# Delta rule in one core: 16x16 diagonal blocks of the inverse by substitution on GpSimd in three of four steps

## The chip, the cores and the metric

The kernel runs on one core of a Trainium2 chip. The metric is the device time of one execution in microseconds (us), lower is better; several runs are timed and their median is taken. Engines are called as in the profile: PE is TensorE, DVE VectorE, ACT ScalarE, POOL GpSimd, SP SyncE, which here only issues DMAs.

## The reference, cut to what matters

The program is two large blocks, one after the other, over 1024 tokens of width 1024: a hybrid of a gated delta rule and dilated attention with a feed-forward part, then a block with two state space branches. Only one piece of the delta rule is touched, run forwards and backwards over the tokens, for 8 heads of 64 values:

```python
kb = k * beta[..., None]
a_low = jnp.where(strict, jnp.einsum('nhcid,nhcjd->nhcij', kb, k) * decay, 0.0)
tmat = lax.linalg.triangular_solve(eye + a_low, eye, left_side=True, lower=True, unit_diagonal=True)
u = jnp.einsum('nhcij,nhcjv->nhciv', tmat, v * beta[..., None])
w = jnp.einsum('nhcij,nhcjk->nhcik', tmat, kb * jnp.exp(g)[..., None])
# then, chunk by chunk: v_new = u - w S; o = q S + (q k^T) v_new; S = decay S + k^T v_new
```

So each chunk needs the inverse `tmat` of a unit triangular matrix I + A. The kernel takes chunks of 128 tokens, so A and its inverse are 128x128.

## The kernel before, in words

Heads are taken in 4 pairs, p = 0 to 3. A pair has 8 chunks in each direction d. A group n = 8 p + s holds chunk s of both directions and both heads, four 128x128 matrices, in a tile that is 128x512. Two groups, called e = 0 and 1, are worked on together; that is a step, m = 0 to 3, so a pair has four steps and the kernel sixteen.

For each pair PE first does four projections of 1024x1024 by 128 columns, the blocks `dn` 0 to 3 (`product`, L303; each matmul is made three times from a high and a low part of its operands, and POOL makes those parts of each weight block in `split`, L249 and L251). Small work of the pair before and of this one is hooked in between their matmuls. Then come the four steps, in which PE does no projection.

Preparation of a group: POOL spreads the log decays (`spread`, L1967), PE sums them (`spread_g`, L1309), DVE and ACT form the exponentials (`exponents`, `exponential`), PE makes k k^T and q k^T (`gram`, L1325), DVE multiplies by the decay (`decayed`), PE transposes (`turn_a`, L1336) and ACT scales into the tile AA (`take_a`, L1610). POOL then forms X = I - A within 2x2 blocks (`first_level`, L1975 and L1979), PE transposes it (`turn_x0`, L1346) and ACT copies it to YY (`take_y0`).

The inverse is then built in NL = 6 levels. Level l turns diagonal blocks of size 2, 4, ... 64 into blocks of twice the size: PE multiplies A by Y (`times_a`, L1364, or L1361 at the last level), DVE masks the product into PM (`masked`, L1803), PE multiplies by X (`times_x`, L1390), DVE subtracts from Y (`corrected`). From level 1 on X is Y transposed anew (`turn_y`, L1377, and ACT's `take_x`, L1623).

Each level of a step has two slots, q = 2 l and 2 l + 1, one behind `times_a` and one behind `times_x`. A function `between(p, m, q)` on PE, ACT and DVE puts other work there: at q = 0 to 5 of steps 1 to 3 the scan of the two groups of the step before (`scan1`, `scan2`, `scan3`: L1264 and L1269, L1281, L1290 and L1297), and at q = 0 to 11 of steps 0 to 2 the preparation of the next step's two groups. Every engine runs its list in order and waits on semaphores. SP's list has only weight loads in this stage; a load waits until POOL has split the block that had the buffer before.

## Time and profile before

| | us |
|---|---|
| median of 3 runs | 3808.23 |
| the runs | 3802.79 to 3814.48 |
| the profiled execution: its own time | 3801.48 |
| the profiled execution: its span | 3799.7 |

| engine | busy us | share of the span |
|---|---|---|
| PE matmul | 3641.7 | 96% |
| PE weight load | 3016.4 | 79% |
| DVE | 1549.1 | 41% |
| POOL | 1297.7 | 34% |
| ACT | 1070.8 | 28% |

The shares are means over the whole program. A time like 1211.88 in the rows further down is us from the start of the span. In a timeline neighbouring instructions of one line are merged: a row gives the start, the time from the start of the first to the end of the last, the count, and in brackets how long the engine was idle before and who released it. Ends of matmuls are modelled and overlap the next start, so distances between starts are used here.

### The profile page before, as it was taken

What the parts mean: (1) busy time and instruction counts of PE and PEld (TensorE: products, weight loads), DVE (VectorE), ACT (ScalarE), POOL (GpSimd) and SP (SyncE); (2) the same over time, 40 slices, a digit from 0 to 9 for tenths busy, and PEclk for the clock granted to TensorE, in tenths of its full rate; (3) what the DMA queues carried; (4) which work ended last, traced back from release to release, by engine and by line L of the source; (5) the groups of instructions that cost most, each with busy time, mean ns of one, the idle gap of its engine ahead of it and who ended that gap; (6) DMA issues with size and microseconds to landing.
All of it is one profiled execution on the core that took longest, in us unless ns stands there. A gap on an engine that the chain in (4) does not pass through costs nothing. (4 is left out here: it accounts for less than half of the span.)

```text
span 3799.7 us, 47903 instructions
## 1 busy us (share of the span) xinstructions
PE 3641.7 (96%) x19176; PEld 3016.4 (79%) x19176; DVE 1549.1 (41%) x2391; ACT 1070.8 (28%) x1817; POOL 1297.7 (34%) x876
## 2 busy tenths in 40 slices
PE   6999999999999999999999999999979999999998
PEld 5777878776898989888877787887867887777877
DVE  4332333343354535444574333333337224444433
ACT  3343333331333333333013111111121114443221
POOL 4221212124221221222345343433342435554543
PEclk9999999999999999999999999999989999999999
DMA  2000000002000000001131111111132111111122
GB/s 98 23 29 27 28 23 33 24 28 76 29 12 12 1 23 1 23 1 60 67 127 59 50 44 50 44 50 44 50 116 70 48 43 49 48 47 46 61 83 72
DMA packets 52699, 173.19 MB, mean 46 GB/s; under 512 B 6569, under 2 KB 13353, under 8 KB 49841
## 3 DMA queue, kind: packets, MB, share of 16 engines
q1 hardware_dynamic: 52528, 170.80, 13.1%
q8 instruction: 122, 2.00, 0.2%
q14 instruction: 49, 0.39, 0.0%
HBM read 151.25 MB, written 19.52 MB: 45 GB/s over the span
## 5 line engine op out<-in xcount | busy, mean ns | idle before, releaser
L303 PE MATMUL DP<-XH,WH 128*128 128x512 f32 x2608 | 896.4, 425 | 21.7 <-POOL WL L251 20.5
L249 POOL CAST WH<-WRAW 128x1024 fp32r<-128x1024 f32 (+2 forms) x257 | 263.8, 1026 | 1638.3 <-issue 1041.5
L303 PE MATMUL DP<-XL,WH 128*128 128x512 f32 x2608 | 812.3, 393 | 0.0
L303 PE MATMUL DP<-XH,WL 128*128 128x512 f32 x2608 | 810.3, 392 | 0.0
L303 PEld LDWEIGHTS DP<-XH,WH 128*128 128x128 f32 x2608 | 475.0, 191 | 180.5 <-issue 86.8
L251 POOL TENSOR_TENSOR WL<-WRAW,WH 128x1024 fp32r<-128x1024 f32 (+2 forms) x257 | 588.5, 2290 | 20.7
L303 PEld LDWEIGHTS DP<-XL,WH 128*128 128x128 f32 x2608 | 494.2, 190 | 107.2
L303 PEld LDWEIGHTS DP<-XH,WL 128*128 128x128 f32 x2608 | 492.7, 189 | 107.1
L836 DVE SCALAR_TENSOR_TENSOR SS<-B,RQ,SBI 128x256 f32<-128x256 f32 (+2 forms) x192 | 74.5, 429 | 380.7 <-PE B L541 380.7
L1975 POOL TENSOR_TENSOR XX<-AA,CON 128x256 f32<-128x256 f32 x64 | 45.4, 731 | 433.4 <-ACT AA L1610 433.4
L1390 PE MATMUL DP<-PM,XX 128*128 128x64 f32 (+1 forms) x1536 | 172.6, 269 | 15.4 <-ACT XX L1623 15.0
L1390 PEld LDWEIGHTS DP<-PM,XX 128*128 128x128 f32 (+1 forms) x1536 | 163.2, 184 | 29.2 <-issue 26.3
L686 ACT ACTIVATE PP<-SS,NM 128x256 f32<-128x256 f32 (+2 forms) x192 | 88.4, 461 | 317.4 <-DVE NM L843 317.4
L1364 PEld LDWEIGHTS DP<-YY,AA 128*128 128x128 f32 x1280 | 151.2, 192 | 13.9 <-issue 13.1
L1364 PE MATMUL DP<-YY,AA 128*128 128x64 f32 x1280 | 156.0, 275 | 4.3 <-ACT YY L1617 4.3
L1623 ACT ACTIVATE XX<-DP 128x512 f32<-128x512 f32 x160 | 86.8, 594 | 237.8 <-PE DP L1377 237.8
L367 DVE TENSOR_TENSOR XR<-XR,B 128x1024 f32<-128x1024 f32 x88 | 106.4, 1219 | 101.5 <-PE B L347 101.5
L2135 DVE SCALAR_TENSOR_TENSOR TG<-DP,COL,TG 128x1023 f32<-128x1023 f32 x44 | 56.5, 1283 | 196.6 <-ACT TG L2123 193.8
L1803 DVE TENSOR_TENSOR PM<-DP,CM 128x256 f32<-128x256 f32 x192 | 81.5, 425 | 129.9 <-PE DP L1364 127.2
L541 PE MATMUL B<-KZA,QA 128*128 128x512 f32 (+2 forms) x192 | 130.6, 768 | 0.0
L2135 DVE SCALAR_TENSOR_TENSOR TU<-DP,COL,TU 128x1023 f32<-128x1023 f32 x44 | 56.4, 1283 | 173.8 <-ACT TU L2123 170.9
L347 PE MATMUL B<-FH,WH 128*128 128x512 f32 x352 | 109.7, 393 | 15.5 <-DVE XR L367 15.5
(461 smaller groups left out, 5497.9 us busy)
## 6 DMA issues: line engine op xcount, KB each, us to landing
WRAW<-in_w_up SPq DMA_DIRECT2D x44, 512.0 KB, 3.2
WRAW<-in_w_attn SPq DMA_DIRECT2D x36, 512.0 KB, 3.2
WRAW<-in_w_down SPq DMA_DIRECT2D x22, 512.0 KB, 3.2
XR<-in_x SPq DMA_DIRECT2D x8, 1024.0 KB, 8.0
WRAW<-in_w_dn SPq DMA_DIRECT2D x16, 512.0 KB, 3.5
WRAW<-in_w_lrux SPq DMA_DIRECT2D x10, 512.0 KB, 3.3
WRAW<-in_w_lrug SPq DMA_DIRECT2D x10, 512.0 KB, 3.2
WRAW<-in_w_bl SPq DMA_DIRECT2D x10, 512.0 KB, 3.5
```

What stands on the lines that cost most here:

```text
L249: pool.tensor_copy(WH[b.slot][:, 0:b.kt, :], WRAW[b.slot][:, 0:b.kt, :]).then_inc(w_hi, 1)
L251: pool.tensor_tensor(WL[b.slot][:, 0:b.kt, :], WRAW[b.slot][:, 0:b.kt, :], WH[b.slot][:, 0:b.kt, :].bitcast(F32), ALU.subtract).then_inc(w ...
L303: mm = pe.matmul(DP[b.slot][:, half * H:half * H + H], w[b.slot][:, k, :], x[:, k, half * H:half * H + H], start=one, stop=end)
L347: mm = pe.matmul(dst[:, half * H:half * H + H], w[b.slot][:, k0 + k, :], x[:, k, half * H:half * H + H], start=one, stop=end)
L367: dve.tensor_tensor(dst[:, m0 + o, :], dst[:, m0 + o, :], (B45, B67)[o % 2][:, :], ALU.add).then_inc(part_read, 1)
L541: pe.matmul(SPS[t % 2][:, 0:2 * w].rearrange("p (h k) -> p h k", h=2), att_tokens(g, t)(QA[i % 2][:, :]), keys, start=True, stop=True).the ...
L686: e = act.activation(PP[t % 2][:, h, 0:w], SS[t % 2][:, h, 0:w], ACT.Exp, scale=0.125, bias=NM[:, g, t, o:o + 1], accum_out=LS[:, g, t, o: ...
L1364: mm = pe.matmul(PT_U[e][:, o:o + 64].rearrange("p (m b) -> p m b", b=2 << l), AA[v][e][:, d, h, :], part(YY[v][e][:, d, h, :], l, 1 - d), ...
L1390: mm = pe.matmul(PT_U[e][c, o:o + 64], XX[v][e][c, d, h, c], PM[e][c, d, h, :], start=True, stop=True)
L1623: act.activation(XX[v][e][:, :, :, :].rearrange("p d h n -> p (d h n)"), PT_X[e], ACT.Copy).then_inc(lx_ready[e], 1)
L1803: dve.tensor_tensor(PM[e][:, :, :, :], PT_U[e][:, 0:256].rearrange("p (d h n) -> p d h n", d=2, h=2), CM[:, l].rearrange("p d (a n) -> p d ...
L2135: dve.scalar_tensor_tensor(out=d, in0=src, scalar=COL[:, ds(f * 2 + (COLS["ffnconv"] + 44 * tap + 22 * part + t), 1)], in1=d, op0=ALU.mult ...
```

## The change

In step 0 of each pair the inverse is built as before, in six levels. In steps 1 to 3 `lowest(n)` is NB = 3: levels 0 to 2 are left out, and levels 3 to 5 start from the inverses of the 16x16 diagonal blocks. These come over a new path, once per step, for the 64 blocks of its two groups:

1. SP (`blocks_sp`) waits for `take_a` of both groups, writes AA (512 KB) to `aa_dram` and waits for its landing.
2. SP issues 8 DMAs of the diagonal blocks back, each 8 blocks of 16 rows of 64 bytes, so that a block lies in one partition of BL or BW.
3. POOL (`base_blocks`) inverts all 64 blocks at once: four instructions of layout, 14 times a multiply and a subtract, and one more of layout. Each waits for the one before it.
4. SP issues 8 DMAs of the blocks into the diagonal of `yy_dram`, waits for them, waits for the scans that still read the YY tile, and loads `yy_dram` (512 KB) into YY. The first `times_a` of the step waits for it.

`first_level`, `turn_x0` and `take_y0` are left for step 0 only. With six slots instead of twelve in steps 1 to 3, the preparation moves: slots 0 to 10 of step 0 make the matrices of steps 1 and 2, step 1 makes those of step 3, and steps 2 and 3 only scan. AA has three buffers instead of two, the q k^T tiles eight instead of six, XX one instead of two. SP has the two first loads of the next pair ahead of the three paths. DVE zeroes a tile that SP writes to `yy_dram` once, behind `st_zero` of pair 0 and ahead of two weight loads. The last fills of MX change places.

```diff
@@ -1059,10 +1059,15 @@
...
-        AA = [[at(f"AA{v}{e}", 112 + 4 * v + 2 * e, [P, 2, 2, P]) for e in range(2)] for v in range(2)]
-        XX = [[at(f"XX{v}{e}", 120 + 4 * v + 2 * e, [P, 2, 2, P]) for e in range(2)] for v in range(2)]
...
+        AAV = [at(f"AA{v}", kb, [P, 2, 2, 2, P]) for v, kb in enumerate((120, 116, 148))]
+        YYV = [at(f"YY{v}", S0 + 38 + 4 * v, [P, 2, 2, 2, P]) for v in range(2)]
...
+        XX = [at(f"XX{e}", S0 + 34 + 2 * e, [P, 2, 2, P]) for e in range(2)]
+        BL, BY, BT, BW = (at(n, 124 + i, [P, 16, 16]) for i, n in enumerate(("BL", "BY", "BT", "BW")))
+        aa_dram = nc.dram_tensor("aa_dram", [P, 8, P], F32, kind="Internal").ap()
+        yy_dram = nc.dram_tensor("yy_dram", [P, 8, P], F32, kind="Internal").ap()
...
@@ -1123,7 +1132,53 @@
...
+        def lowest(n):
+
+            return 0 if n // 2 % 4 == 0 else NB
...
+        def diagonal(dram, q):
+
+            return bass.AP(dram.tensor, dram.offset + P * q, ap=[[16 * (8 * P + 1), 8], [8 * P, 16], [1, 16]])
+
+        def blocks_sp(sp, g):
+
+            c, v, m = chain(g), g % 2, g % 4
+            sp.wait_ge(aa_ready, 2 * g + 2)
+            sp.dma_start(aa_dram, AAV[m][:, :, :, :, :].rearrange("p d e h n -> p (d e h) n")).then_inc(aa_out, 16)
+            sp.wait_ge(aa_out, AA0 + 16 * (c + 1))
+            sp.wait_ge(yy_out, YYO0 + 128 * c)
+            for q in range(8):
+                t = BW if q >= 4 else BL
+                sp.dma_start(t[8 * q:8 * q + 8, :, :], diagonal(aa_dram, q)).then_inc(blk_in, 16)
+            if c:
+                sp.wait_ge(yy_in, YYI0 + 16 * c)
+            sp.wait_ge(blk_ready, RDY0 + c + 1)
+            for q in range(8):
+                t = BW if q >= 4 else BY
+                sp.dma_start(diagonal(yy_dram, q), t[8 * q:8 * q + 8, :, :]).then_inc(yy_out, 16)
+            sp.wait_ge(yy_out, YYO0 + 128 * (c + 1))
+            sp.wait_ge(v_ps, 2 * g - 2)
+            sp.dma_start(YYV[v][:, :, :, :, :].rearrange("p d e h n -> p (d e h) n"), yy_dram).then_inc(yy_in, 16)
...
@@ -1169,13 +1224,13 @@
...
-            sp.dma_start(MX[:, 2:4, :], mx_dram[:, 2:4, :]).then_inc(mx_in[1], 16)
+            for i in range(2):
...
-            sp.dma_start(MX[:, 4:6, :], mx_dram[:, 4:6, :]).then_inc(mx_in[2], 16)
...
             sp.wait_ge(qkv_ready, NGRP)
-            sp.dma_start(MX[:, 0:2, :], mx_dram[:, 0:2, :]).then_inc(mx_in[0], 16)
+            sp.dma_start(MX[:, 4:6, :], mx_dram[:, 4:6, :]).then_inc(mx_in[2], 16)
...
@@ -1339,38 +1396,40 @@
...
             def times_a(n, l):
                 p, s, e, v = grp(n)
                 if l == 0:
-                    pe.wait_ge(y0_ready, n + 1)
-                if n // 2 * NL + l:
-                    pe.wait_ge(ly_ready[e], n // 2 * NL + l)
+                    pe.wait_ge(y0_ready, n // 8 * 2 + e + 1)
+                elif l == lowest(n):
+                    pe.wait_ge(yy_in, YYI0 + 16 * (chain(n // 2) + 1))
+                if levels_done(n, l):
+                    pe.wait_ge(ly_ready[e], levels_done(n, l))
...
@@ -1493,32 +1552,35 @@
                         scan2(a + 1)
                     if q == 5:
                         scan3(a + 1)
-                if m < 3:
-                    n = NT * p + 2 * m + 2
-                    if q == 0:
-                        spread_g(n)
+                n = NT * p + 2 * m + 2
+                if m == 0 and q < 11:
+                    i, k = q // 6 * 2, q % 6
+                    if k == 0:
+                        spread_g(n + i)
+                        spread_g(n + i + 1)
+                    if k in (2, 3):
+                        gram(n + i, k - 2)
+                    if k == 4:
+                        turn_a(n + i)
+                        turn_a(n + i + 1)
+                if m == 1:
                     if q == 1:
-                        spread_g(n + 1)
-                    if q == 3:
-                        gram(n, 0)
+                        spread_g(n + 2)
+                        spread_g(n + 3)
+                    if q in (3, 4):
+                        gram(n + 2, q - 3)
                     if q == 5:
-                        gram(n, 1)
-                    if q == 7:
-                        turn_a(n)
-                        turn_a(n + 1)
-                    if q == 10:
-                        turn_x0(n)
-                    if q == 11:
-                        turn_x0(n + 1)
+                        turn_a(n + 2)
+                        turn_a(n + 3)
             for p in range(NPAIR):
                 if p:
                     for e in range(2):
-                        pe.wait_ge(lx_ready[e], 5 * 4 * p)
+                        pe.wait_ge(lx_ready[e], TV * p)
                 product(pe, Block("dn", p, 0), XH, XL, within=scans_first(p))
                 if p:
                     for e in range(2):
-                        pe.wait_ge(ly_ready[e], NL * 4 * p)
+                        pe.wait_ge(ly_ready[e], LV * p)
                 product(pe, Block("dn", p, 1), XH, XL, within=scans_last(p))
                 product(pe, Block("dn", p, 2), XH, XL, within=during_v(p))
                 product(pe, Block("dn", p, 3), XH, XL, within=during_z(p))
@@ -1529,19 +1591,20 @@
...
                 for m in range(4):
                     a = NT * p + 2 * m
-                    for l in range(NL):
+                    for l in range(lowest(a), NL):
+                        q = 2 * (l - lowest(a))
                         times_a(a, l)
                         times_a(a + 1, l)
                         if l:
                             turn_y(a, l)
                             turn_y(a + 1, l)
-                        between(p, m, 2 * l)
+                        between(p, m, q)
                         times_x(a, l)
                         times_x(a + 1, l)
-                        between(p, m, 2 * l + 1)
+                        between(p, m, q + 1)
...
@@ -1907,6 +1976,8 @@
...
+                if p == 0:
+                    dve.memset(YYV[1][:, :, :, :, :], 0.0)
                 dve.memset(SB[:, :, :], 0.0).then_inc(st_zero, 1)
...
@@ -1960,24 +2032,56 @@
                 p, s, e, v = grp(n)
                 if n >= 2:
-                    pool.wait_ge(dec_ready, 2 * n - 2)
+                    pool.wait_ge(dec_ready, 4 * (n // 2))
                 for d in range(2):
                     i = 8 * d + 2 * p
                     g = ABN[:, chunk(s, d), i:i + 2].rearrange("p (h k) -> p h k", k=1).broadcast_to([P, 2, P])
                     x = pool.tensor_tensor(RB[e][:, d], twice(con("tri", d, P)), g, ALU.mult)
                 x.then_inc(rb_ready, 1)
+            def step(p, c, i):
+
+                return 2 * (p + 1) + NSTEP * c + i
+
             def first_level(n):
                 p, s, e, v = grp(n)
+                k = step(p - 1, 3 * p, e + 1)
                 pool.wait_ge(aa_ready, n + 1)
                 for d in range(2):
-                    x = pool.tensor_tensor(XX[v][e][:, d], AA[v][e][:, d], twice(con("m0", d, P)), ALU.mult)
+                    x = pool.tensor_tensor(XX[e][:, d], aa(n)[:, d], twice(con("m0", d, P)), ALU.mult)
                 x.then_inc(x0_part, 1)
-                pool.wait_ge(x0_part, n + 1)
+                pool.wait_ge(x0_part, k)
                 for d in range(2):
-                    x = pool.tensor_tensor(XX[v][e][:, d], twice(IDENT), XX[v][e][:, d], ALU.subtract)
+                    x = pool.tensor_tensor(XX[e][:, d], twice(IDENT), XX[e][:, d], ALU.subtract)
                 x.then_inc(x0_ready, 1)
+
+            def base_blocks(g):
+
+                p, c = g // 4, chain(g)
+                lo, up = slice(0, 32), slice(32, 64)
+                pool.wait_ge(blk_in, BLK0 + 128 * (c + 1))
+                pool.tensor_scalar(BY[lo, :, :], BL[lo, :, :].rearrange("p i j -> p j i"), -1.0, None, ALU.mult).then_inc(
+                    blk_step, 1)
+                pool.wait_ge(blk_step, step(p, c, 1))
+                pool.wait_ge(rb_ready, min(NT * p + 2 * (g % 4) + 4, NGRP))
+                pool.tensor_scalar(BY[up, :, :], BW[up, :, :], -1.0, None, ALU.mult).then_inc(blk_step, 1)
+                pool.tensor_copy(BL[up, :, :], BW[up, :, :].rearrange("p i j -> p j i")).then_inc(blk_step, 1)
+                pool.wait_ge(blk_step, step(p, c, 3))
+                pool.tensor_copy(BY[0:64, :, :].rearrange("p i j -> p (i j)")[:, 0:256:17], ONES[0:64, 0:16]).then_inc(
+                    blk_step, 1)
+                pool.wait_ge(blk_step, step(p, c, 4))
+                for j in range(1, 15):
+                    y = BY[0:64, 0:j, j + 1:16]
+                    t = BT[0:64, 0:j, j + 1:16]
+                    pool.tensor_tensor(t, BY[0:64, 0:j, j:j + 1].broadcast_to([64, j, 15 - j]),
+                                       BL[0:64, j + 1:16, j:j + 1].rearrange("p i a -> p a i").broadcast_to(
+                                           [64, j, 15 - j]), ALU.mult).then_inc(blk_step, 1)
+                    pool.wait_ge(blk_step, step(p, c, 2 * j + 3))
+                    pool.tensor_tensor(y, y, t, ALU.subtract).then_inc(blk_step, 1)
+                    pool.wait_ge(blk_step, step(p, c, 2 * j + 4))
+                pool.tensor_copy(BW[up, :, :], BY[up, :, :].rearrange("p i j -> p j i")).then_inc(blk_ready, 1)
+                pool.wait_ge(blk_ready, RDY0 + c + 1)
             def add_other(n):
@@ -2007,12 +2104,20 @@
...
-                for m in range(4):
-                    prepare(NT * p + 2 * m)
-                add_other(NT * p + 4)
-                add_other(NT * p + 5)
                 for i in range(2):
+                    first_level(NT * p + i)
+                for i in range(2, 4):
+                    spread(NT * p + i)
+                for m in range(1, 4):
+                    for n in range(NT * p + 2 * m + 2, min(NT * p + 2 * m + 4, NGRP)):
+                        spread(n)
+                    base_blocks(4 * p + m)
+                for i in range(2):
+                    if i:
+                        for e in range(2):
+                            pool.wait_ge(lp_ready[e], levels_done(NT * p + 4 + e, NL))
                     split(pool, Block("dn", p + 1, i) if p < NPAIR - 1 else Block("mixga", 0, i))
+                    add_other(NT * p + 4 + i)
...
@@ -2534,11 +2639,18 @@
                     load(sp, Block("dn", 0, i), a["w_dn"])
                     mx_spill(sp, 6 + i)
                 sp.dma_start(CM[:, :, :, :], a["levels"]).then_inc(cm_in, 16)
+                sp.wait_ge(st_zero, 1)
+                sp.dma_start(yy_dram, YYV[1][:, :, :, :, :].rearrange("p d e h n -> p (d e h) n")).then_inc(yy_out, 16)
                 for p in range(NPAIR):
-                    for i in range(0 if p else 2, 4):
+                    for i in range(2, 4):
                         load(sp, Block("dn", p, i), a["w_dn"])
-                for i in range(2):
-                    load(sp, Block("mixga", 0, i), a["w_gatea"], i)
+                    for i in range(2):
+                        if p < NPAIR - 1:
+                            load(sp, Block("dn", p + 1, i), a["w_dn"])
+                        else:
+                            load(sp, Block("mixga", 0, i), a["w_gatea"], i)
+                    for m in range(1, 4):
+                        blocks_sp(sp, 4 * p + m)
                 mx_fill(sp)
                 for i, w in enumerate(("w_dnout", "w_gatea")):
                     load(sp, Block("mixa", 0, i), a[w], 2 * i)```

SP's list in pair 0, before. Behind these rows only weight loads follow up to the fills of MX.

```order
L241 DMA WRAW_54<-in_w_dn 128x1024
L1166 DMA mx_dram<-GB_101 128x1024
L2536 DMA CM<-in_levels 128x768
L241 DMA WRAW_53<-in_w_dn 128x1024
L241 DMA WRAW_54<-in_w_dn 128x1024
```

The same list now, from the second pair of weight loads on, the path of step 1 and the beginning of that of step 2.

```order
L241 DMA WRAW_53<-in_w_dn 128x1024
L241 DMA WRAW_54<-in_w_dn 128x1024
L1167 DMA aa_dram<-AA_121 128x1024
L1172 DMA BL<-aa_dram 8x16x16 x4
L1172 DMA BW<-aa_dram 8x16x16 x4
L1178 DMA yy_dram<-BY 8x16x16 x4
L1178 DMA yy_dram<-BW 8x16x16 x4
L1181 DMA YY_124<-yy_dram 128x1024
L1167 DMA aa_dram<-AA_122 128x1024
```

A path is 18 DMAs in one list, and the next path stands behind the last of them.

PE's list in pair 0, before: the last level of step 0 and the first of step 1. XX_126 and XX_127 are what `first_level` made for step 1.

```order
L1361 MATMUL DP<-YY_128,AA_120 64x64 x4
L1361 MATMUL DP<-YY_129,AA_121 64x64 x4
L1377 MATMUL DP<-CON,YY_128 128x128 x4
L1377 MATMUL DP<-CON,YY_129 128x128 x4
L1346 MATMUL B<-CON,XX_126 128x128 x4
L1390 MATMUL DP<-PM_138,XX_124 64x64 x4
L1390 MATMUL DP<-PM_139,XX_125 64x64 x4
L1346 MATMUL B<-CON,XX_127 128x128 x4
L1364 MATMUL DP<-YY_130,AA_122 128x64 x4
L1364 MATMUL DP<-YY_131,AA_123 128x64 x4
```

The same place now. YY_124 is the tile that SP loads, and the row with it is the first of step 1.

```order
L1420 MATMUL DP<-YY_123,AA_120 64x64 x8
L1436 MATMUL DP<-CON,YY_123 128x128 x8
L1393 MATMUL B<-CON,DQX 128x128 x8
L1449 MATMUL DP<-PM_137,XX_125 64x64 x4
L1449 MATMUL DP<-PM_138,XX_126 64x64 x4
L1423 MATMUL DP<-YY_124,AA_121 128x64 x8
L1436 MATMUL DP<-CON,YY_124 128x128 x8
L1319 MATMUL B<-SB,KQ 128x128 x2
L1324 MATMUL B<-SB,KQ 128x128 x2
```

The last level of step 0 now holds the `turn_a` of step 2 (L1393), the `turn_x0` are gone, and the first scan stands behind the row that waits.

## Rows read from the trace of the kernel before

**Rows 1.** Windows, pair 1: length; PE, PEld, DVE, ACT, POOL busy; clock; DMA share, GB/s.
```profile
1211.88:1245.86 33.98, 32.46 (x272) 29.65 (x273) 15.27 (x41) 10.76 (x23) 8.15 (x13) 0.95 0.00 1
1245.86:1283.32 37.46, 36.63 (x331) 34.45 (x329) 20.27 (x63) 14.94 (x41) 7.89 (x13) 1.00 0.00 1
1283.32:1320.78 37.46, 36.63 (x330) 34.45 (x329) 20.28 (x63) 13.99 (x40) 7.90 (x13) 1.00 0.01 1
1320.78:1352.73 31.95, 30.75 (x290) 29.67 (x289) 14.91 (x46) 10.29 (x29) 10.99 (x10) 1.00 0.10 34
```

**Rows 2.** Timeline of PE, levels 1 to 5 of step 3, pair 1.
```profile
1326.15 1.95 PE L1364 MATMUL DP<-YY,AA 128*128 128x64 f32 x16
...
1332.83 1.90 PE L1364 MATMUL DP<-YY,AA 128*128 128x64 f32 x16
...
1339.41 1.95 PE L1364 MATMUL DP<-YY,AA 128*128 128x64 f32 x16
...
1342.59 1.97 PE L1390 MATMUL DP<-PM,XX 128*128 128x64 f32 x16 [0.34 <-ACT XX L1623]
1344.39 1.95 PE L1364 MATMUL DP<-YY,AA 128*128 128x64 f32 x16
...
1349.47 1.03 PE L1361 MATMUL DP<-YY,AA 64*64 64x64 f32 x16
...
1352.73 0.73 PE L303 MATMUL DP<-XH,WH 128*128 128x512 f32 x2
```

**Rows 3.** Timeline of PE, step 0 of pair 1.
```profile
1218.00 1.08 PE L1309 MATMUL B<-RB,CON 128*128 128x256 f32 x4
1218.91 1.89 PE L1364 MATMUL DP<-YY,AA 128*128 128x64 f32 x16
...
1223.93 1.14 PE L1325 MATMUL B<-KQ 64*128 64x256 f32 x8
1225.00 2.00 PE L1364 MATMUL DP<-YY,AA 128*128 128x64 f32 x16
...
1236.20 1.04 PE L1336 MATMUL B<-CON,DQX 128*128 128x128 f32 x8
1237.09 1.90 PE L1364 MATMUL DP<-YY,AA 128*128 128x64 f32 x16
```

**Rows 4.** Timeline of ACT, the same step.
```profile
1236.85 2.18 ACT L1610 ACTIVATE AA<-B,PSC 128x128 f32<-128x128 f32 x8 [2.11 <-PE B L1336]
```

**Rows 5.** DMA issues by line: count, KB each, median us to landing.
```profile
WRAW<-in_w_attn SPq DMA_DIRECT2D x36, 512.0 KB, 3.2
...
mx_dram<-GB SPq DMA_DIRECT2D x8, 512.0 KB, 2.9
...
MS<-kp_dram SPq DMA_DIRECT2D x64, 32.0 KB, 1.9
...
kp_dram<-KS SPq DMA_DIRECT2D x8, 32.0 KB, 1.6
```

**Rows 6.** Timeline of SP, DMAs issued one behind another.
```profile
2864.68 7.62 SPq L2715 DMA_DIRECT2D MS<-kp_dram  x16
```

**Rows 7.** Groups of POOL, shapes apart: count, busy us, mean ns, idle before.
```profile
L1975 POOL TENSOR_TENSOR XX<-AA,CON 128x256 f32<-128x256 f32 x64 | 45.4, 731 | 433.4 <-ACT AA L1610 433.4
...
L1989 POOL TENSOR_TENSOR OQ<-OQ,OD 128x128 f32<-128x128 f32 x32 | 14.0, 458 | 153.0 <-ACT OQ L1580 153.0
...
L926 POOL TENSOR_SCALAR SBI<-BX,CON 128x256 f32<-128x256 f32 x8 | 7.4, 932 | 0.0
...
L249 POOL CAST WH<-WRAW 128x256 fp32r<-128x256 f32 x10 | 5.0, 498 | 10.7 <-PE DP L303 10.7
```

**Rows 8.** Timeline of POOL, L1979 waits for the result of L1975.
```profile
1030.72 1.42 POOL L1975 TENSOR_TENSOR XX<-AA,CON 128x256 f32<-128x256 f32 x2 [23.91 <-ACT AA L1610]
1032.21 1.41 POOL L1979 TENSOR_TENSOR XX<-CON,XX 128x256 f32<-128x256 f32 x2
```

**Rows 9.** Timeline of PE, its return after an idle stretch in another stage.
```profile
2789.23 1.19 PE L333 MATMUL DP<-XH,WH 128*128 128x512 f32 x2 [4.98 <-POOL XL L444]
```

**Rows 10.** Windows, the stretch behind that return.
```profile
2789.23:2793.60 4.37, 4.37 (x10) 3.44 (x11) 2.45 (x2) 1.88 (x2) 4.22 (x2) 0.50 0.87 375
```

More of the change, by code:

```diff
@@ L1720, in delta_act @@
                     a = NT * p + 2 * m
-                    for l in range(NL):
+                    for l in range(lowest(a), NL):
+                        q = 2 * (l - lowest(a))
                         if l:
@@ L1939, in delta_dve @@
                     a = NT * p + 2 * m
-                    for l in range(NL):
+                    for l in range(lowest(a), NL):
+                        q = 2 * (l - lowest(a))
                         masked(a, l)
                         masked(a + 1, l)
-                        between(p, m, 2 * l)
+                        between(p, m, q)
                         corrected(a, l)
                         corrected(a + 1, l)
-                        between(p, m, 2 * l + 1)
+                        between(p, m, q + 1)
             a, b = NGRP - 2, NGRP - 1
```

139 lines of the change are left out of this document (78 added, 61 removed).

## The prediction

> **What bounds the kernel now.** I read the windows of the four steps of one pair first, then the timeline of PE inside a step, then who feeds it. In the four steps of pair 1 PE is busy 136.5 of 140.85 us (33.98 + 37.46 + 37.46 + 31.95), DVE, ACT and POOL at most 54% of any step [rows 1]. The timeline shows the same from within: PE goes from one list item to the next and waits only 0.34 us per level, for ACT's copy of the transposed X [rows 2]. So a step costs what PE's instructions cost, and no projection runs beside it. Whatever leaves PE's list in a step shortens the program, as long as nothing later than PE takes over. The other pairs look alike, so I work out pair 1 and take it four times.
>
> **What PE's list loses.** Step 3 has only scans between its levels. Its six levels take, by distances between `times_a` starts, 5.37 (from 1320.78, where the last window of [rows 1] begins, to 1326.15), 6.68, 6.58, 4.98, 5.08 and 3.26 us [rows 2]. Level 2 has scan work and level 3 has none but a 0.34 us wait, so one level's scan work is 6.58 - 4.98 + 0.34 = 1.94. Eight transposes take 0.89 (1236.20 to 1237.09), two matmuls of `spread_g` for one group 0.91 (1218.00 to 1218.91), a `gram` 1.07 (1223.93 to 1225.00) [rows 3].
>
> - New steps 2 and 3: the first level with a `turn_y` that level 0 did not need, 5.37 + 0.89; then 6.68; then the small last level with scans in its slots, 3.26 - 0.34 + 1.94. Sum 17.8.
> - New step 1: the same and one preparation, 2 x 0.91 + 2 x 1.07 + 0.89 = 4.85. Sum 22.7.
> - New step 0: 33.98, less `turn_x0` (0.89), plus the second preparation (4.85). Sum 37.9.
>
> PE's work is then 96.2 us a pair instead of 140.85, 44.7 less. If nothing took over, the program would lose 179 us.
>
> **What takes over: the path through memory.** Call L the time from `take_a` of a step to YY landed. Nothing in it is PE's, and SP and POOL do it in order. Its parts:
>
> - AA out, 512 KB: 2.9 to landing, as `mx_dram<-GB` [rows 5].
> - 8 DMAs of blocks in: SP issues 16 DMAs in 7.62 us, 0.476 each [rows 6], so the last is issued 3.3 behind the first, and lands 1.9 later, as `MS<-kp_dram` [rows 5]. 5.2.
> - POOL, below: 12.5.
> - 8 DMAs out: 3.3, and 1.6 as `kp_dram<-KS` [rows 5]. 4.9.
> - YY in, 512 KB: 3.2 as the weight loads [rows 5].
> - Five handovers between SP, DMA and POOL, of which the trace shows only one kind, POOL to itself (0.07, below). I take 0.6 for all.
>
> POOL runs 28 dependent instructions of 14 to 56 elements, 1120 in all. No such small one is in the trace. 128x256 takes 0.731 and 128x128 0.458 [rows 7], so 2.13 ns an element and 0.185 fixed. A dependent one starts 0.07 behind the end of its predecessor (1030.72 + 1.42 = 1032.14, next at 1032.21) [rows 8]. So 28 x 0.255 + 1120 x 0.00213 = 9.5. Around them stand two negations of 256 elements, between 0.50 and 0.93 each [rows 7], I take 0.7; two copies of 256 at 0.50; a small one; with gaps 3.0. Together 12.5. From below: the fixed part could be nothing but the gap, 28 x 0.07 + 2.4 + 2.0 = 6.4. From above: each small one costs what 128x128 costs, 28 x 0.53 + 3.7 = 18.5, and farther, what 128x256 costs, 28 x 0.80 + 3.7 = 26.1. I take the line through both rows, since the work shrinks with the elements in them.
>
> L is 2.9 + 5.2 + 12.5 + 4.9 + 3.2 + 0.6 = 29.3 us.
>
> **The pair with the path in it**, from the start of step 0:
>
> - AA of step 1 is ready behind level 0 (7.03, from 1211.88 to 1218.91), level 1 with a second `gram` in it (6.09 + 1.07), `times_a` and `turn_y` (1342.59 - 1339.41 - 0.34 = 2.84) [rows 2, 3] and `turn_a` with ACT's copy (1236.20 to 1239.03, 2.83) [rows 3, 4]: at 19.9. Step 1 starts at 19.9 + L = 49.2, where PE was done at 37.9: 11 us of waiting. It ends at 71.9.
> - SP reaches the path of step 2 when it has issued YY of step 1, 2.8 before that lands: step 2 starts at 17.1 + 2 L = 75.7, a wait of 4.
> - AA of step 3 is ready 1.9 behind the end of step 1, at 44.5 + L = 73.8, while SP is free at 14.3 + 2 L = 72.9. Step 3 starts at 44.5 + 2 L = 103.1, where step 2 ended at 93.5: 10 us of waiting. The pair ends at 62.3 + 2 L = 120.9. Above L = 30.2 SP is the later one and it is 32.1 + 3 L.
>
> Queued behind the waiting `times_a` is everything else of PE, the scans too, so DVE and ACT wait with it and nothing fills the gap. After an idle stretch of 4.98 us PE came back at granted clock 0.50 and stayed there 4.4 us [rows 9, 10]. At half speed that loses at most 2.2; in two long waits a pair I take 1.5 each, 3 together. So 123.9 instead of 140.85, 17 less a pair, 68 less in all.
>
> **Parts at nothing.** The levels that leave DVE (masks and subtractions) and ACT (`take_x`) do not bound. DVE's and ACT's share of two preparations in step 0 falls into slots of 3 us each where both are under half busy [rows 1]; if one is late, PE loses tenths. The fills of MX still follow the scans. POOL's `split` of the next pair's first weights, some 3.4 us, now stands behind the last path, but POOL is done with that 8 us before step 3 begins, and its `add_other` is then on time; if it were not, the next projection would wait. In pair 0 two weight loads wait for `st_zero`, behind the first projection: about 1 us, once.
>
> The profiled execution took 3801.5: less 68, plus 1, 3735. The median of the runs is 6.7 above it, so I say 3738.
>
> **A rule on small pieces.** The DMA batches above are priced with packets of 512 bytes, at 32 KB a DMA; the new ones are 8 KB in pieces of 64 bytes. The Trainium skill (DMA: Bandwidth & Descriptors, Specifications) puts 512 B as the least for full rate and says that below it the engines read, modify and write. The same page (Rules for kernel authors) says that a transfer whose outermost dimension is under 16 uses only that many engines, here 8. No run here shows either for such pieces. By these rules both batches would come later than I count, and the time would be that of the first rival, 3770 to 3810, where by the rows it is 3738.
>
> **Rivals.**
>
> - Small pieces are slow. If the 8 DMAs out take twice the 0.476 each, L is 32.6 and a pair 32.1 + 97.8 + 3 = 132.9, 8 less than before: 3770. For: the nearest rows have pieces eight times as large, and nothing shows what a small one costs when written. Against: they land in 1.6 and 1.9 us, mostly a constant it seems. Twice for both batches gives L = 36 and about 3810.
> - The path is shorter. With POOL at its lower end L is 23.2, a pair 62.3 + 46.4 + 3 = 111.7, 29 less: 3685. For: POOL's durations are rough, and part of the 0.185 may overlap.
> - Slower than before: POOL's substitution. The place is the 28 dependent instructions. If one costs 0.66, midway between the dependent 128x128 (0.53) and 128x256 (0.80), POOL takes 21.8, L is 38.6 and a pair 147.9 + 3 = 150.9, 10 more: 3842. It decides from L = 35.3 on, that is from 0.54 an instruction, just above the 128x128 price. For: three-dimensional accesses with rows of 1 to 14 elements are nowhere in the trace. Against: size does count in both rows.
> - The waits come but fall together with what PE gains, so that it comes out even. Only a narrow band of L near 35 does this.
>
> **How the numbers follow.** My forecast, L between 27 and 32, has 0.45 and its own range 3715 to 3765; the short path 0.18; small pieces 0.12; POOL slow 0.18; even 0.07. From the first three, 0.75 for faster. Within 0.3% (11 us, about what a measurement of this kernel can tell from no change) 0.07, slower 0.18. The range goes from 3690, most of the short path, to 3825, half of the slow case.
>
> **What would show it.** Right: PE idle before the first `times_a` of steps 1 to 3 by about 11, 4 and 10 us, released by a DMA; 28 POOL instructions in 9.5 us; steps of 18 us between waits. Wrong: no such idle time, or POOL instructions over 0.54 us apart, or the batches of 8 DMAs landing more than 6 us behind their first issue.

## The result and the profile after

| | us |
|---|---|
| after: median of 4 runs | 3746.56 (3741.84 to 3751.26) |
| before: median of 4 runs | 3808.21 (3802.79 to 3814.48) |
| ratio after / before | 0.984, 95% interval 0.9822 to 0.9858 |
| profiled execution: its own time, span | 3747.99, 3746.2 |

The change makes the kernel 1.6% faster, 62 us. The page's line of busy time: PE is busy 137 us less than before (3641.7), and only 53.5 us of it are gone from the span (3799.7).

```profile
PE 3504.7 (94%) x17736; PEld 2884.9 (77%) x17736; DVE 1484.5 (40%) x2248; ACT 1033.5 (28%) x1745; POOL 1361.4 (36%) x1176
```

The four steps of pair 1 as windows, in the columns of [rows 1]. The bounds are the starts of the first `times_a` of each step and of the next projection.

```profile
1208.74:1255.07 46.33, 33.81 (x297) 30.82 (x297) 20.55 (x58) 14.63 (x33) 16.08 (x42) 0.90 0.13 35
1255.07:1281.37 26.30, 26.05 (x209) 24.52 (x209) 14.00 (x46) 9.42 (x29) 12.29 (x36) 0.85 0.13 31
1281.37:1311.47 30.10, 17.73 (x177) 17.20 (x177) 11.35 (x39) 9.02 (x30) 15.22 (x37) 0.87 0.18 55
1311.47:1332.22 20.75, 20.34 (x177) 19.95 (x177) 9.17 (x31) 7.62 (x24) 7.37 (x7) 0.86 0.09 31
```

The pair takes 123.5 us where it took 140.85. PE is busy 97.9 of them. Two windows hold 12 us in which it does nothing, and the granted clock is no longer 1.00 in the steps behind. The timeline of PE names what it waited for, at steps 1, 2 and 3:

```profile
1255.07 3.67 PE L1423 MATMUL DP<-YY,AA 128*128 128x64 f32 x16 [12.39 <-DMA YY<-yy_dram]
...
1281.37 2.00 PE L1423 MATMUL DP<-YY,AA 128*128 128x64 f32 x16 [0.25 <-DMA YY<-yy_dram]
...
1311.47 3.68 PE L1423 MATMUL DP<-YY,AA 128*128 128x64 f32 x16 [11.97 <-DMA YY<-yy_dram]
```

In the list of waits, over all pairs (total us, times, longest), it is the largest of PE:

```profile
PE DP L1423 <- DMA YY<-yy_dram: 96.9, 12, 12.4
```

SP's timeline shows the path of step 1. YY landed at 1255.07, so the path is 28.55 long from its first row. The last row is already the next path: its 512 KB go out while YY still comes in. YY took 4.27 us here, against 3.36 in path 2, where nothing was issued behind it before it landed, and this second AA took 5.10 us to its landing instead of 2.62.

```profile
1226.52 0.33 SPq L1167 DMA_DIRECT2D aa_dram<-AA  x1
1229.14 1.39 SPq L1172 DMA_DIRECT2D BL<-aa_dram  x4
1230.58 1.42 SPq L1172 DMA_DIRECT2D BW<-aa_dram  x4
1246.78 1.37 SPq L1178 DMA_DIRECT2D yy_dram<-BY  x4
1248.20 1.44 SPq L1178 DMA_DIRECT2D yy_dram<-BW  x4
1250.80 0.34 SPq L1181 DMA_DIRECT2D YY<-yy_dram  x1
1251.19 0.43 SPq L1167 DMA_DIRECT2D aa_dram<-AA  x1
```

POOL in the gap between reads and writes: the layout, the first pair, the longest and the last of the 28 instructions that depend on each other.

```profile
1233.32 1.07 POOL L2064 TENSOR_SCALAR BY<-BL 32x256 f32<-32x256 f32 x1 [8.26 <-DMA BW<-aa_dram]
...
1236.33 0.21 POOL L2077 TENSOR_TENSOR BT<-BY,BL 64x14 f32<-64x14 f32 x1
1236.62 0.21 POOL L2081 TENSOR_TENSOR BY<-BY,BT 64x14 f32<-64x14 f32 x1
...
1241.18 0.32 POOL L2077 TENSOR_TENSOR BT<-BY,BL 64x56 f32<-64x56 f32 x1
...
1245.82 0.23 POOL L2081 TENSOR_TENSOR BY<-BY,BT 64x14 f32<-64x14 f32 x1
1246.11 0.60 POOL L2083 COPY BW<-BY 32x256 f32<-32x256 f32 x1
```

### The profile page after: what moved, and what is told of

It reads as the page before. It is cut to its first block and busy times, and to the rows that moved or that the text cites. A ratio compares the mean times of both kernels' runs of the same rounds, so it can differ in the third digit from the quotient of the medians.

```text
span 3746.2 us, 45340 instructions
## 1 busy us (share of the span) xinstructions
PE 3504.7 (94%) x17736; PEld 2884.9 (77%) x17736; DVE 1484.5 (40%) x2248; ACT 1033.5 (28%) x1745; POOL 1361.4 (36%) x1176
## 5 line engine op out<-in xcount | busy, mean ns | idle before, releaser
L303 PE MATMUL DP<-XH,WH 128*128 128x512 f32 x2608 | 900.7, 427 | 23.0 <-POOL WL L251 23.0
L249 POOL CAST WH<-WRAW 128x1024 fp32r<-128x1024 f32 (+2 forms) x257 | 264.2, 1028 | 1647.1 <-issue 1039.9
L303 PE MATMUL DP<-XL,WH 128*128 128x512 f32 x2608 | 814.7, 394 | 0.0
L303 PE MATMUL DP<-XH,WL 128*128 128x512 f32 x2608 | 813.2, 393 | 0.0
L303 PEld LDWEIGHTS DP<-XH,WH 128*128 128x128 f32 x2608 | 477.2, 192 | 182.8 <-issue 86.1
L303 PEld LDWEIGHTS DP<-XL,WH 128*128 128x128 f32 x2608 | 496.5, 190 | 108.1
L303 PEld LDWEIGHTS DP<-XH,WL 128*128 128x128 f32 x2608 | 494.3, 190 | 107.5
L1423 PE MATMUL DP<-YY,AA 128*128 128x64 f32 x704 | 99.9, 302 | 101.0 <-DMA YY<-yy_dram 96.9
L1423 PEld LDWEIGHTS DP<-YY,AA 128*128 128x128 f32 x704 | 95.3, 217 | 105.4 <-DMA YY<-yy_dram 98.9
L1686 ACT ACTIVATE XX<-DP 128x512 f32<-128x512 f32 x112 | 61.7, 595 | 214.8 <-PE DP L1436 213.9
L347 PE MATMUL B<-FL,WH 128*128 128x512 f32 x352 | 108.6, 390 | 0.0
L347 PE MATMUL B<-FH,WL 128*128 128x512 f32 x352 | 108.4, 389 | 0.0
L1870 DVE TENSOR_TENSOR PM<-DP,CM 128x256 f32<-128x256 f32 x120 | 48.9, 422 | 148.9 <-PE DP L1423 148.8
L1449 PEld LDWEIGHTS DP<-PM,XX 128*128 128x128 f32 (+1 forms) x960 | 93.5, 179 | 5.6 <-issue 4.6
## 6 DMA issues: line engine op xcount, KB each, us to landing
WRAW<-in_w_up SPq DMA_DIRECT2D x44, 512.0 KB, 3.5
WRAW<-in_w_attn SPq DMA_DIRECT2D x36, 512.0 KB, 3.5
WRAW<-in_w_down SPq DMA_DIRECT2D x22, 512.0 KB, 3.5
WRAW<-in_w_dn SPq DMA_DIRECT2D x16, 512.0 KB, 3.5
aa_dram<-AA SPq DMA_DIRECT2D x12, 512.0 KB
YY<-yy_dram SPq DMA_DIRECT2D x12, 512.0 KB, 3.5
WRAW<-in_w_lrux SPq DMA_DIRECT2D x10, 512.0 KB, 3.6
```

What stands on the lines that cost most here:

```text
L249: pool.tensor_copy(WH[b.slot][:, 0:b.kt, :], WRAW[b.slot][:, 0:b.kt, :]).then_inc(w_hi, 1)
L303: mm = pe.matmul(DP[b.slot][:, half * H:half * H + H], w[b.slot][:, k, :], x[:, k, half * H:half * H + H], start=one, stop=end)
L347: mm = pe.matmul(dst[:, half * H:half * H + H], w[b.slot][:, k0 + k, :], x[:, k, half * H:half * H + H], start=one, stop=end)
L1423: mm = pe.matmul(PT_U[e][:, o:o + 64].rearrange("p (m b) -> p m b", b=2 << l), aa(n)[:, d, h, :], part(YY[v][e][:, d, h, :], l, 1 - d), st ...
L1449: mm = pe.matmul(PT_U[e][c, o:o + 64], XX[e][c, d, h, c], PM[e][c, d, h, :], start=True, stop=True)
```

## The experiments

A measured time is the median of its runs, the ratio is to the kernel before as it ran beside that variant. "Pair" in this section is from the last projection matmuls ahead of step 0 to the first behind step 3, some 2.5 us more than from the start of step 0. It is 126.1, 126.1, 125.6 and 125.7 in the changed kernel, mean 125.9. Names of functions are those of the changed kernel; each edit is against it.

**The path taken away (e1).**

```diff
-                    for m in range(1, 4):
-                        blocks_sp(sp, 4 * p + m)
...
-                    base_blocks(4 * p + m)
...
-                elif l == lowest(n):
-                    pe.wait_ge(yy_in, YYI0 + 16 * (chain(n // 2) + 1))
```

> Leaves out the whole path (both crossings through memory and the substitution): steps 1 to 3 start from whatever stands in YY, so that part of the inverse is not computed; PE's work is that of the changed kernel. Theory (the path alone makes the waits, and the waits make the clock fall): a pair shrinks from 123.5 us to the PE work alone, 33.9 + 22.7 + 17.8 + 17.8 = 92.2, so 31.3 x 4 = 125 us less than the changed kernel's 3747: about 3622, no idle of PE over 2 us in the steps. Rival (the other engines' small work, now squeezed into half as many slots, holds PE as well): steps 2 and 3 stay at 22 us or more, waits on ACT, DVE or POOL show in them, and the time is 3650 or more.

Measured 3620.27 us, ratio 0.9514 (0.9496 to 0.9533). Windows of its pair 1:

```profile
1166.58:1202.66 36.08, 35.50 (x297) 32.11 (x297) 20.00 (x57) 12.99 (x30) 4.96 (x9) 0.95 0.00 1
1202.66:1224.88 22.22, 22.22 (x208) 20.95 (x209) 14.16 (x46) 10.54 (x31) 1.21 (x3) 1.00 0.01 2
1224.88:1242.75 17.87, 17.46 (x178) 17.07 (x177) 10.61 (x38) 9.45 (x32) 4.65 (x5) 1.00 0.10 31
1242.75:1260.64 17.89, 17.48 (x178) 17.09 (x178) 10.17 (x35) 7.51 (x24) 7.38 (x7) 1.00 0.10 32
```

The time is the 3622 expected. The steps are what PE's list costs, and the other engines keep up with six slots as they did with twelve. Of the 188 us that shorter lists give, the path and the lower clock behind its waits take 126 back.

**The path made shorter and longer (e2, e3).** First the substitution away, then each of its multiplies made three times:

```diff
-                for j in range(1, 15):
-                    ...
```

> Leaves out the 28 multiplies and subtracts of the substitution; the path keeps its DMAs and layout, so the diagonal blocks are wrong. Theory (the path is one chain in which every us counts): a path goes from 28.7 to 19.0 us, step 1 starts at 17.7 + 19 = 36.7 after step 0, 2.8 behind its end; step 2 without a wait; step 3 at the end of step 1 (60.7) + 19 = 80; pair about 99 instead of 123.5, total 3747 - 98 = 3649, and the full rate comes back since no wait is long. Rival (the DMAs make the wait, the substitution lies beside them): under 40 us less, 3707 or more. The Trainium skill's rule of small DMA pieces would be the rival's reason.

```diff
+                    for r in range(3):
                         pool.tensor_tensor(t, BY[0:64, 0:j, j:j + 1].broadcast_to([64, j, 15 - j]),
...
```

> Every multiply of the substitution is made three times over (28 more dependent instructions, same result), which lengthens a path by about 28 x 0.35 = 9.7 us to 38.4. Theory (three paths in a row set the pair; my slower rival decided from L = 35.3 on): steps 1 to 3 start at 17.7 + L, + 2L, + 3L = 56, 94.5, 133, pair 153.6, 30 more than now: total 3747 + 120 = 3867, slower than before (3808). Rival (two paths set the pair, as my formula 62.3 + 2L had it): 19.5 more a pair, 3825. Third (a path overlaps the one before on other queues): under 3800.

Measured 3656.26 (ratio 0.9593, 0.9569 to 0.9617) and 3859.03 (1.0134, 1.0114 to 1.0155). First rows of PE behind its waits in pair 1 of the shorter one, then of the longer one:

```profile
1222.65 2.32 PE L1423 MATMUL DP<-YY,AA 128*128 128x64 f32 x16 [2.67 <-DMA YY<-yy_dram]
...
1267.46 2.71 PE L1423 MATMUL DP<-YY,AA 128*128 128x64 f32 x16 [2.63 <-DMA YY<-yy_dram]
```

```profile
1295.44 3.68 PE L1423 MATMUL DP<-YY,AA 128*128 128x64 f32 x16 [22.29 <-DMA YY<-yy_dram]
...
1332.41 3.67 PE L1423 MATMUL DP<-YY,AA 128*128 128x64 f32 x16 [10.97 <-DMA YY<-yy_dram]
...
1369.63 3.68 PE L1423 MATMUL DP<-YY,AA 128*128 128x64 f32 x16 [15.20 <-DMA YY<-yy_dram]
```

Without the substitution waits of 2.7, 0 and 2.6 are left, expected were 2.8, 0 and 2: the chain with its slack is right on the short side. The full rate did not come back as expected, though: the granted clock is 0.93 in step 1 and 0.91 in step 3, and from the start of step 0 pair 1 took 102.7 us where some 99 were expected. On the long side the wait ahead of step 1 grew by 9.9 and the distances between step starts are 37.0 and 37.2, no longer the 26.3 and 30.1 of the windows above. Together 27.7 a pair, three times the added 9.9 less the slack that step 3 had. The last step is 1.2 longer, 28.9 in all. So from here each us of path costs 2.9 a pair, over eleven in all (112 for 9.9). By a straight line between these two measurements, which is an estimate, the program passes the 3808 of before when 5.4 of the 9.9 are added (62 of 112), at L of 34.0. Spread over 28 instructions that is 0.19 on top of 0.35, or 0.54 us each.

**PE kept busy while it waits (e4, e7).** 12, then 14 matmuls of constants ahead of the wait in steps 1 and 3:

```diff
+                    if e == 0 and n // 2 % 2:
+                        pe.wait_ge(lx_ready[0], turns_done(n, l))
+                        for i in range(12):
+                            pe.matmul(PT_X[0], ONES, CON[:, 0:512], start=True, stop=True)
                     pe.wait_ge(yy_in, YYI0 + 16 * (chain(n // 2) + 1))
```

> Ahead of the wait for YY in steps 1 and 3, PE makes 12 matmuls of constants (128x512, about 0.85 us each, 10.2 in all) into a bank that nobody reads, so it is busy in the 12 us that it waits. Theory (what follows the wait at half the clock costs 3.4 to 3.7 us per long wait, and falls because PE stood still): the full clock stays, steps 1 and 3 take 22.7 and 17.8; step 1's gain comes back through AA of step 3 for only 1.4, step 3's fully: 4.8 a pair, 19 us less: about 3727. Rival (the clock falls for the power of the whole stretch, not for the pause, or the dummies push the start of the steps back): 3745 or more.

Measured 3735.02, ratio 0.9812 (0.9792 to 0.9833), which overlaps the changed kernel's; 3727 was expected. Its pairs are 123.4, 125.3, 123.2 and 126.0, mean 124.5: 1.4 each or 6 in all, where 19 were expected. Its profiled execution is another 6.7 us shorter ahead of pair 0's step 0 and 4.2 behind pair 3, where the edit does nothing, so I don't count these. PE stood still 2 us behind the constants, and the rows behind are part at full rate and part at half.

> As e4_warm, with 14 matmuls of constants instead of 12 (12.3 us instead of 10.6), so that PE stands still for under 0.5 us ahead of steps 1 and 3, where 2 us were left. Theory (a pause of 2 us still brings half the clock for 3.4 or 6.8 us): those windows go, each worth 1.7 to 3.4 us of PE's time: 3735 becomes 3723 to 3729. Rival (they come from the step's own gaps or the power of the stretch): 3735 as before.

Measured 3749.96, ratio 0.984 (0.982 to 0.986): no gain at all, though the clock is back. Windows of step 1, of the wait behind it and of step 2, pair 1:

```profile
1250.44:1272.83 22.39, 22.39 (x208) 20.88 (x208) 13.76 (x45) 9.06 (x28) 12.04 (x35) 1.00 0.08 14
1272.83:1276.74 3.91, 0.00 (x0) 0.00 (x0) 1.47 (x6) 1.77 (x7) 1.21 (x3) 0.84 0.55 197
1276.74:1297.34 20.60, 20.19 (x176) 19.80 (x177) 9.18 (x31) 7.62 (x24) 12.32 (x35) 0.87 0.08 20
```

Step 1 takes 22.39 instead of 26.05 us for the same instructions, so a long wait costs 3.7 by the clock. Ahead of step 2 all of it came back as a wait for YY, which took the clock of step 2 with it. The path of step 3 did gain, because the matrices that it starts from are made in step 1: its AA went out 70.4 behind the start of step 0 instead of 74.2, and its YY was issued at 96.2 instead of 98.9. This gain could not be seen in the time, because of what follows. Ahead of step 3 the constants ran from 1297.34 for 12.2 us, past the landing of its YY (issued 1300.40, and such a load took 3.4 to 4.3), and held the step up by about 5, to 105.2 behind the start of step 0 instead of 102.7. Both expectations missed: I had counted the clock as if PE set step 2's start, and the constants as if they ended ahead of each landing.

**Weight loads first (e5).**

```diff
-                sp.wait_ge(st_zero, 1)
-                sp.dma_start(yy_dram, YYV[1][:, :, :, :, :].rearrange("p d e h n -> p (d e h) n")).then_inc(yy_out, 16)
                 for p in range(NPAIR):
                     for i in range(2, 4):
                         load(sp, Block("dn", p, i), a["w_dn"])
+                    if p == 0:
+                        sp.wait_ge(st_zero, 1)
+                        sp.dma_start(yy_dram, YYV[1][:, :, :, :, :].rearrange("p d e h n -> p (d e h) n")).then_inc(yy_out, 16)
```

> In pair 0, SP issues the two weight loads of blocks 2 and 3 ahead of the wait for the zeroed tile and its write to memory, not behind them; nothing else moves. Theory (the 6.1 us that pair 0 starts late are this queue's, the 1 us that I gave it was too little): 5 us back, about 3742. Rival (other work, the slower clock there): the same as the changed kernel, 3747. Third (the write of zeros then comes so late that the first path waits): over 3747.

Measured 3743.16, ratio 0.9824 (0.9804 to 0.9844): in the direction expected, but inside the changed kernel's interval. The mechanism is plain in the rows. POOL's split of block 2 in pair 0 in the changed kernel, and PE's wait for a split behind it:

```profile
978.21 1.04 POOL L249 CAST WH<-WRAW 128x1024 fp32r<-128x1024 f32 x1 [19.97 <-DMA WRAW<-in_w_dn]
```

```profile
981.72 0.74 PE L303 MATMUL DP<-XH,WH 128*128 128x512 f32 x2 [2.56 <-POOL WL L251]
```

With the loads first POOL waits for PE there, 15 us earlier, and PE for nobody between 957 and its wait of 0.96 us for step 0's first YY:

```profile
962.99 1.04 POOL L249 CAST WH<-WRAW 128x1024 fp32r<-128x1024 f32 x1 [9.33 <-PE DP L303]
```

From the `spread_g` matmuls that stand ahead of these projections (957.14 in the changed kernel, 952.58 here) to step 0 it is 59.90 us in the changed kernel and 53.82 here, exactly what it was before the change. So the order of SP's list costs 6.1 in that profile: 2.7 up to 981.72, the wait, and 3.4 behind it, where PE ran at granted clock 0.89 (32.09 us for what took 28.72). The second part is not certain to come: in two of the eight profiles with the late loads, e6 and e7, the wait is there and the clock stays at 1.00 behind it. In all four profiles without the wait (before, e5, e9, e10) this stretch takes 28.7 us. That step 0 starts at 1006.40 instead of 1017.04 is more than 6.1, because the `spread_g` itself was 4.6 earlier, ahead of the edit.

**Smaller blocks (e6).** NB = 2, the substitution in 128 blocks of 8x8:

```diff
-        NL, NB = 6, 3
+        NL, NB = 6, 2
...
-            return bass.AP(dram.tensor, dram.offset + P * q, ap=[[16 * (8 * P + 1), 8], [8 * P, 16], [1, 16]])
+            return bass.AP(dram.tensor, dram.offset + P * q, ap=[[8 * (8 * P + 1), 16], [8 * P, 8], [1, 8]])
...
-                for j in range(1, 15):
+                for j in range(1, 7):
```

> Substitution in 8x8 blocks instead of 16x16: 12 dependent instructions of up to 12 elements in each of 128 partitions instead of 28, pieces of 32 bytes instead of 64 and twice as many, and steps 1 to 3 have four levels instead of three. Theory (the path's length is the price): the substitution takes 12 x 0.29 = 3.5 instead of 9.7, the layout about 2 less, L = 20.5; step 1 starts at 17.7 + 20.5 = 38.2 after step 0, 4.3 behind its end; each step is 5.0 longer (as a level without a scan in rows 2); steps 2 and 3 don't wait: pair 38.2 + 27.7 + 22.8 + 22.8 = 111.5, and 1.5 for the clock, 10.5 less than now: 3747 - 42 = 3705. Rival (the count of pieces is what a crossing costs): both crossings take twice as long, L = 28 or more, the gain of the substitution is gone and the added levels stay: pair 126 or more, 3755 or above.

Measured 3725.54, ratio 0.9775 (0.9752 to 0.9798): 21 us less than the changed kernel, where 42 were expected. SP's timeline, path of step 1 in pair 1 (YY landed at 1236.75):

```profile
1214.70 0.33 SPq L1167 DMA_DIRECT2D aa_dram<-AA  x1
1217.32 1.75 SPq L1172 DMA_DIRECT2D BL<-aa_dram  x4
1219.11 1.85 SPq L1172 DMA_DIRECT2D BW<-aa_dram  x4
1227.80 1.72 SPq L1178 DMA_DIRECT2D yy_dram<-BY  x4
1229.57 1.87 SPq L1178 DMA_DIRECT2D yy_dram<-BW  x4
1232.55 0.34 SPq L1181 DMA_DIRECT2D YY<-yy_dram  x1
```

The path is 22.05, 20.5 expected. Twice the pieces made the writes, from first issue to YY's, 4.75 instead of 4.02: 0.7, not twice. The waits of PE were 5.9 ahead of step 1 and none later, steps 2 and 3 took 22.8 and 22.5 as expected. Step 1 took 32.4 and not 27.7: the half clock, 4.7 where I had 1.5 for it. And AA of step 1 was ready 19.5 behind step 0's start, not 17.7: its first `spread_g` ran at half rate, 3.38 us instead of 1.94. That happened in pairs 1 and 3; in pairs 0 and 2 it was 17.8.

**Step 3's preparation moved into the pause (e8 to e10).** On PE (ACT and DVE alike):

```diff
                 if m == 1:
-                    if q == 1:
+                    if q == -1:
                         spread_g(n + 2)
                         spread_g(n + 3)
-                    if q in (3, 4):
-                        gram(n + 2, q - 3)
-                    if q == 5:
+                        gram(n + 2, 0)
+                    if q == 1:
+                        gram(n + 2, 1)
+                    if q == 2:
                         turn_a(n + 2)
...
+                        if q == 0 and m == 1:
+                            between(p, m, -1)
                         times_a(a, l)
```

> The preparation of step 3's two groups is taken out of step 1: sums, exponentials and the first gram go ahead of the first times_a of step 1, so into PE's 12 us pause, the rest into its slots 1 and 2 instead of 3 to 5. SP's list and the substitution stay. Theory (three paths in one queue set the pair, 17.7 + 3L): step 1 starts at 46.3 after step 0 as now, takes 18 to 19 instead of 26, and all of that comes back as a wait ahead of step 2, whose YY is at 17.7 + 2L = 72.6; only the 1.2 us that path 3 now waits for its AA are won, and about 1 of clock: pair 121.5 instead of 123.5, 3747 - 8 = 3739. Rival (PE's work counts while it waits elsewhere): 5 us of PE's work a pair hidden in the pause, 3747 - 20 = 3727 or less.

Measured 3737.60, ratio 0.9819 (0.9795 to 0.9844). Pairs 125.8, 125.4, 125.2, 124.9: 0.6 less each, not the 2 I gave it, and the ratio's interval overlaps the changed kernel's. That the time meets the 3739 expected is luck: of the 13.5 us by which its profile is shorter, 3.6 stand ahead of pair 0's step 0 and 6.0 behind pair 3. Part of the missing gain is again step 0: in pairs 1 and 2 `spread_g` ran at half rate and AA of step 1 was ready 1.7 later, 0.8 on the mean of four pairs. Also, path 3 now starts 0.4 behind the YY issue of path 2, as path 2 did behind path 1's, and its AA takes 5.2 us to go out while that YY comes in. So work hidden in the pause is worth little while the paths set the pair.

> 8x8 blocks as in e6_8x8, with the early preparation of e8_early and the weight loads first of e5_loads_first. Theory (with a path of 22 us PE bounds steps 2 and 3, so work taken out of step 1 is won): e6_8x8's pair of 121.9 between the last and the next projection loses 5 us of PE's work in step 1 and about 3 of its 4.5 at half the clock, 8 x 4 = 32, and 5 for pair 0's loads: 3725 - 37 = 3688. Rival (as in e7_warm_longer, a shorter step 1 waits for path 2): step 2 waits 5 us or more, 3715.

Measured 3703.02, ratio 0.9724 (0.97 to 0.9748), 22 less than e6. Here PE bounds, and the same edit pays: pairs of 116.5, 114.2, 116.6 and 115.7, where e6 had 120.2, 121.9, 120.0 and 122.7. That is 5.4 each where 8 were expected, 5 for work and 3 for the clock. The work was overcounted. The edit takes two `spread_g` and one `gram` out of step 1 (2 x 0.91 + 1.07 = 2.9 us by [rows 3]); the second `gram` and the `turn_a` stay in it. The rest is clock. In pair 1, step 1 took 24.89 us at granted clock 1.00:

```profile
1225.13:1250.02 24.89, 24.23 (x233) 23.23 (x233) 13.56 (x43) 10.79 (x34) 6.44 (x21) 1.00 0.20 52
```

In e6 it took 32.37 at 0.87, so 4.6 of the 7.5 are the clock's. In pairs 0 and 2 step 1 took 28.0 at 0.88, where e6 had 32.0 and 31.4, and only some 0.8 of the difference are.

The last one also changes SP's order, with 16x16 blocks:

```diff
                 sp.dma_start(t[8 * q:8 * q + 8, :, :], diagonal(aa_dram, q)).then_inc(blk_in, 16)
+            if m < 3:
+                sp.wait_ge(blk_in, BLK0 + 128 * (c + 1))
+                aa_sp(sp, g + 1)
```

> 16x16 blocks, e8_early's preparation and e5_loads_first's loads, and SP's list changed: AA of the next path is written to memory as soon as this path's blocks have been read, while POOL works on them, so paths overlap. Theory (path 2 then no longer needs L behind path 1): step 1 starts at 46.3, reads of path 2 follow path 1's YY at once, YY of step 2 at 69.5 and of step 3 at 92 after step 0: pair 92 + 18 = 110, with 2 for the clock 112 instead of 123.5: 3747 - 46 - 5 = 3696. Rival (queues: the 512 KB writes and reads side by side slow each other, or YY's load waits for the scans of two steps before): pair 118 or more, 3720 or above.

Measured 3695.36 (3684.06 to 3703.7), ratio 0.9701 (0.9674 to 0.9728), with 3696 expected. SP's timeline, AA of step 2 now goes out while POOL works on step 1:

```profile
1212.44 1.39 SPq L1177 DMA_DIRECT2D BL<-aa_dram  x4
1213.87 1.42 SPq L1177 DMA_DIRECT2D BW<-aa_dram  x4
1227.20 0.34 SPq L1166 DMA_DIRECT2D aa_dram<-AA  x1
1230.13 1.37 SPq L1186 DMA_DIRECT2D yy_dram<-BY  x4
1231.55 1.43 SPq L1186 DMA_DIRECT2D yy_dram<-BW  x4
1234.20 0.34 SPq L1189 DMA_DIRECT2D YY<-yy_dram  x1
1234.64 1.37 SPq L1177 DMA_DIRECT2D BL<-aa_dram  x4
```

The waits ahead of steps 2 and 3 are 2.6 and 2.2 in pair 1, pairs are 119.0, 115.2, 119.2 and 115.2, mean 117.1. From step 0's start a pair is 114.5, so 8.7 less than in the changed kernel and not the 11.5 expected. The time was met all the same, because step 0 of pair 0 began 9.6 earlier in its profile, where 5 were expected, and because this profiled execution is the slowest of its five runs. It and e9 beat both kernels; between the two the intervals overlap, and e9's pairs are the shorter ones (mean 115.7).

## Why the prediction was right

- **PE's list loses**: right. Steps of 17.8 and 22.7 were measured as 17.9 and 22.2 where nothing waits (e1). Step 0 took 33.9 (46.33 less the wait of 12.39), 37.9 said. The base was too long by 1.7: pair 1's step 0 in [rows 1] ran at granted clock 0.95 and took 33.98, where pairs 0 and 2 took 32.32 at 1.00, and the changed kernel's ran at 1.00. Idle time of 1.5 us in it (33.98 less 32.46 busy) is 0.1 now, filled by the second preparation, and I had counted that on top. It cost nothing, since PE waits behind step 0 anyway.
- **The path L**: 28.6 against 29.3, with errors that cancel. AA out took 2.6 (2.9 said), the reads 4.2 (5.2), POOL 13.5 (12.5), the writes 4.0 (4.9), YY in 4.3 (3.2). The two batches are shorter because SP issues a DMA every 0.355 us and not every 0.476 [rows 6]. In POOL the 28 instructions took 9.8 as the line through both rows said (9.5); the layout on 32 partitions took 1.07 and 0.84 for negations and 0.60 for copies.
- **The pair**: step starts at 46.3, 72.6 and 102.7 behind that of step 0, said 49.2, 75.7 and 103.1. AA of step 1 was ready 2.1 earlier than I had it; 1.7 of them are level 0, 5.32 us at full clock and not the 7.03 of [rows 3] at 0.76. The waits were 12.4, 0.25 and 12.0, said 11, 4 and 10. Step 2's wait is short because step 1 ran at the lower clock and reached just to YY. The pair's 123.5 against 123.9 is partly luck: AA of step 1 came 2.1 sooner and two paths were 1.5 shorter together, which hid that the clock cost about 2.6 more than I gave it.
- **The clock**: this is the term of the pair that was mis-sized. A long wait costs 3.7 in step 1 (26.05 against e7's 22.39) and 2.9 in step 3 (20.75 against e1's 17.89), said 1.5 each. The return row [rows 9, 10] showed 4.4 us at half; here waits of 12 us were followed by 7.6 in step 1 and 5.9 in step 3. Step 3's part counts in full. Step 1's part lies beside path 2 but ahead of path 3, whose AA is made in step 1: SP had been free since 1278.35 and issued it at 1282.91. With the clock kept up (e7) YY of step 3 was issued 2.7 sooner. So some 5.6 of the 6.5 count, where I had 3.
- **Sum**: from step 0 of pair 0 to the projection behind pair 3, 765.6 us became 697.3 (1006.19 to 1771.75, now 1017.04 to 1714.38): 68 less, as forecast, by errors that cancel as above. The profiled execution is 3748.0 and not 3735. Outside this stretch it grew by 14.8, where I had 1. Ahead of pair 0 stand 10.9: 4.8 of them are there at 957, before anything that changed, and 6.1 in pair 0's projections. There I had 1 for `st_zero`, the other term that was mis-sized: SP's write of zeros waits until DVE comes to `st_zero`, and two loads stand behind it (e5 shows the wait gone). Another 3.9 come behind pair 3 (2027.9 before, 2031.8 now). In the profiles of the ten variants, which have the same code there, this part takes 2025.9 to 2037.9, so 3.9 is no more than executions differ by. And the last step of the sum has a slip: 3735 and 6.7 are 3741.7 and not 3738. That the median fell by 62 and the profiled execution by 53.5 is where each lies among its runs.
- **Rivals.** The short path: POOL took 13.5 and not the 6.4 of its lower end, and L was 28.6, not 23.2. Coming out even: that needs L near 34 to 35. Small pieces: the batches landed in 4.2 and 4.0, faster than the priced ones, so the Trainium skill's rule (DMA: Bandwidth & Descriptors, Specifications) shows nothing at 1024 pieces of 64 bytes in this trace; at 2048 of 32 bytes a batch took 0.7 more. No run here shows whether each crossing used only 8 engines. The slower case: its mechanism is real and near. It decides at L of 34 (said 35.3), at 0.54 us an instruction (said 0.54); measured were 0.35. (The forecast of that rival has 3.3 us around the 28 instructions, where the text says 3.0 and 3.7; this moves its threshold by 0.01 us an instruction.) The step from two paths a pair to three, which I put at L = 30.2, was 1.6 above the L that came out.
